# Differential attention on one core: value and output tiles turned in 32x32 squares by VectorE instead of 128x128 by TensorE

## What is computed

```
h = rms_norm(x, norm_pre) * (1 + scale) + shift           # scale, shift, gate from silu(c) @ ada_w + ada_b
q, k, v, z = h @ w_in                                      # four slices of 2048 columns
p1, p2 = softmax(q1 k1' * s), softmax(q2 k2' * s)          # chunk-causal mask, chunks of 64
o = (p1 - lam * p2) @ v                                    # per head, 256 wide
o = rms_norm(o, subln) * (1 - lambda_init) * silu(z)
out = x + gate * rms_norm(o @ w_out, norm_post)
```

## Time and profile before

| what | value |
|---|---|
| device time, median of 3 runs | 1906.76 us (1906.63 to 1907.32) |
| profiled execution, its own time | 1907.34 us |
| profiled execution, span of the trace | 1905.5 us |
| PE busy | 1866.0 us (98%) |
| DVE busy | 1379.5 us (72%) |
| ACT busy | 810.1 us (43%) |
| POOL busy | 794.4 us (42%) |
| DMA queue of SP, share of 16 engines | 76.4% |

### The profile page before, as it was taken

How to read it: one execution, slowest core, us unless ns; L and a number is a source line. 1 busy time by engine, 2 the same in 40 slices (tenths; PEclk the granted TensorE clock), 3 DMA queues, 4 the chain that set the end, 5 groups by cost and what they waited for, 6 DMA issues and landing times.

```text
span 1905.5 us, 26384 instructions
## 1 busy us (share of the span) xinstructions
PE 1866.0 (98%) x9072; PEld 1540.9 (81%) x9072; DVE 1379.5 (72%) x2028; ACT 810.1 (43%) x1516; POOL 794.4 (42%) x844
## 2 busy tenths in 40 slices
PE   4999999999999999999999999999999999999998
PEld 1488888888888888888888888888888888888886
DVE  3687888886655546787887877878778776569467
ACT  5633333333444433444443444444444445546452
POOL 2076565655644523344344434434443422116023
PEclk9999999999999999999999999999999999999999
DMA  9898898886674698786877778686777679657777
GB/s 354 253 313 279 274 297 278 284 290 232 214 267 160 237 356 263 225 250 192 253 229 227 235 216 252 198 254 212 232 240 221 213 228 291 207 186 257 258 240 265
DMA packets 394048, 473.16 MB, mean 248 GB/s; under 512 B 22614, under 2 KB 268476, under 8 KB 391228
## 3 DMA queue, kind: packets, MB, share of 16 engines
q1 hardware_dynamic: 393632, 471.43, 76.4%
q10 hardware_dynamic: 284, 0.05, 0.0%
HBM read 323.54 MB, written 147.86 MB: 247 GB/s over the span
## 4 chain that ended last, share of the span: by engine, by line
PE 93%; DVE 1%; DMA 1%; ACT 0%; issue 0%; SPq 0%; POOL 0%; DVEq 0%; POOLq 0%; ACTq 0%
PE ps L1752 30%; PE ps L1754 30%; PE ps L1753 30%; PE ps L1885 2%; PE ps L1861 1%; PE ps L1904 1%; PE ps L1721 0%; DMA ubf<-s_dr 0%; DMA z_dr<-cc 0%; PE ps L1833 0%; DVE ring L1310 0%; ACT h L1040 0%; DVE xt L1632 0%; DVE tB L1330 0%; DVE tB L1327 0%
## 5 line engine op out<-in xcount | busy, mean ns | idle before, releaser
L1752 PE MATMUL ps<-blk,ring 128*128 128x512 f32 x1524 | 603.3, 396 | 2.6 <-DVE blk L1357 1.9
L1754 PE MATMUL ps<-blk,ring 128*128 128x512 f32 x1524 | 594.6, 390 | 0.0
L1753 PE MATMUL ps<-blk,ring 128*128 128x512 f32 x1524 | 594.2, 390 | 0.0
L1752 PEld LDWEIGHTS ps<-blk,ring 128*128 128x128 f32 x1524 | 286.3, 188 | 66.0 <-issue 9.7
L1754 PEld LDWEIGHTS ps<-blk,ring 128*128 128x128 f32 x1524 | 286.0, 188 | 60.8
L1753 PEld LDWEIGHTS ps<-blk,ring 128*128 128x128 f32 x1524 | 286.5, 188 | 55.8
L1310 DVE TENSOR_TENSOR ring<-sums,ring 128x512 fp32r<-128x512 f32 x256 | 234.7, 917 | 95.5 <-ACT ring L1006 93.6
L836 POOL TENSOR_TENSOR sums<-raw 128x512 f32<-128x512 f32 x128 | 191.5, 1496 | 226.9 <-DVE ring L1310 206.0
L1006 ACT ACTIVATE ring<-sums 128x512 fp32r<-128x512 f32 x256 | 160.6, 628 | 179.3 <-PE ps L1754 175.6
L1310 DVE TENSOR_TENSOR ring<-raw,ring 128x512 fp32r<-128x512 f32 x192 | 179.2, 934 | 58.9 <-ACT ring L1006 58.5
L836 POOL TENSOR_TENSOR sums<-sums,raw 128x512 f32<-128x512 f32 x128 | 190.2, 1486 | 20.8 <-DVE ring L1310 14.3
(11 more groups left out here) (159 smaller groups left out, 3181.7 us busy)
## 6 DMA issues: line engine op xcount, KB each, us to landing
raw<-in_diff_w_in_dram SPq DMA_DIRECT2D x64, 1024.0 KB, 7.8
d_dr<-cc SPq DMA_DIRECT2D x124, 256.0 KB, 3.2
cc<-d_dr SPq DMA_DIRECT2D x124, 256.0 KB, 4.1
ubf<-s_dr SPq DMA_DIRECT2D x113, 256.0 KB, 5.0
ada<-in_ada_w_dram SPq DMA_DIRECT2D x88, 256.0 KB, 7.3
tb<-in_diff_w_out_dram SPq DMA_DIRECT2D x32, 512.0 KB, 5.5
t_dr<-tb SPq DMA_DIRECT2D x32, 512.0 KB, 4.9
ada<-in_ada_w_dram SPq DMA_DIRECT2D x32, 512.0 KB
```

The source lines that it names most:

```text
L1752: MM(dst, a_hi, b_hi, start=start, stop=False, skip_group_check=True)
L1753: MM(dst, a_hi, b_lo, start=False, stop=False, skip_group_check=True)
L1754: return MM(dst, a_lo, b_hi, start=False, stop=stop, skip_group_check=True)
```

## The change

Nothing is transposed across the whole of 128 partitions any more. DVE's transpose turns each square of 32x32 in its place, and the DMAs put the squares where they belong.

- `v_turn` is now a DVE instruction of 512 columns from `cc` into bank VX, one slot after the product, in `posts`; `v_dr` keeps rows of 512 tokens, so the stores of values have runs of 2 KB where they had 512 bytes. `load_v` is four DMAs of 32 partitions, each of 16 x 32 runs of 128 bytes, and is issued after the block's first slot.
- `o_turn` is gone from PE. `gate` transposes `o_sb` with a DVE instruction of 256 columns and multiplies by `z_sb` with one instruction; the factor `subln` is now `sub_row`, multiplied in `out_scale`.
- `ozf` and `osum` are one tile `o_all`. `store_pair` is four DMAs of 32 partitions, each 32 x 32 runs of 128 bytes; in the blocks of the first seven heads two of them are issued ahead of the first slot and two ahead of the second slot of the odd block after the pair's second one.
- `load_z` is four DMAs of 8 x 32 runs of 128 bytes, issued by ACT in those blocks (by SP in the last head).

```diff
-        v_dr = dram("v_dr", [HEADS * SEQ, 2, VD])
+        v_dr = dram("v_dr", [HEADS * 2, 2, 2, P, HALF])
-        s_dr = dram("s_dr", [8, HEADS, P, PAIRS, P])
+        s_dr = dram("s_dr", [HEADS, 8 * P, PAIRS, P])
...
             def load_v(h, qb):
-                sp.dma_start(v_sb[:, qb].bitcast(F32),
-                             v_dr[h * SEQ + qb * P:h * SEQ + (qb + 1) * P]).then_inc(v_ld[qb % 2], 16)
+                for c in range(0, P, SIDE):
+                    n = qb % HT * P + c
+                    sp.dma_start(v_sb[c:c + SIDE, qb].rearrange("i s (c j) -> i (s c) j", j=SIDE).bitcast(F32),
+                                 v_dr[h * 2 + qb // HT, :, :, :, n:n + SIDE].rearrange(
+                                     "s m (c i) j -> i (s m c) j", i=SIDE)).then_inc(v_ld[qb % 2], 16)
...
-            def store_pair(h, p):
+            def store_pair(h, p, pieces=range(0, P, SIDE)):
                 sp.wait_ge(ozf_ok, h * NB + 2 * p + 2)
-                sp.dma_start(s_dr[0:4, h, :, p].rearrange("o p n -> p o n"),
-                             ozf.rearrange("p i m n -> p (i m) n")).then_inc(s_st, 16)
                 sp.wait_ge(osum_ok, 4 * (h * PAIRS + p + 1))
-                sp.dma_start(s_dr[4:8, h, :, p].rearrange("o p n -> p o n"), osum[:, :, :]).then_inc(s_st, 16)
+                for c in pieces:
+                    sp.dma_start(s_dr[h, :, p, c:c + SIDE].rearrange("(o j) i -> j o i", j=SIDE),
+                                 o_all[c:c + SIDE].rearrange("j o (b i) -> j (o b) i", i=SIDE)).then_inc(s_st, 16)
...
-                    load_v(h - 1, qb)
                     load_qk(*divmod(a + 1, NB))
-                    for _ in range(sum(SPREAD[qb])):
+                    for k in range(sum(SPREAD[qb])):
+                        if a > 1 and a % 2 and k < 2:
+                            store_pair((a - 2) // NB, (a - 2) % NB // 2, (0, SIDE) if k == 0 else (2 * SIDE, 3 * SIDE))
                         slot(n)
                         n += 1
+                        if k == 0:
+                            load_v(h - 1, qb)
...
-                    load_z(h - 1, qb)
-                    if a and a % 2 == 0:
-                        store_pair((a - 1) // NB, (a - 1) % NB // 2)
...
+            def v_turn(n):
+                i, pi = divmod(n, NP)
+                h, o = head_part(i)[0], AT[pi]
+                if h or o:
+                    dve.wait_ge(post_d, 12 * h + o if o else 12 * (h - 1) + 4)
+                dve.wait_ge(ev_d, 3 * GP + NP * (i - GP) + pi + 1)
+                V.transpose(ps[:, VX], cc[:, buffer_of(i, BLOCK[pi])]).then_inc(vt_ok, 1)
...
             def gate(h, qb):
                 a = h * NB + qb
+                dve.wait_ge(o_ok, a + 1)
+                V.transpose(ps[:, OB, VD:2 * VD], o_sb[:, :]).then_inc(oT_done, 1)
+                dve.wait_ge(z_ld, (a + 1) * 16 * (P // SIDE))
+                if a > 1:
+                    dve.wait_ge(s_st, PAIR_STORED * (a // 2))
                 dve.wait_ge(oT_done, a + 1)
-                dve.wait_ge(z_ld, (a + 1) * 16)
-                if a > 1:
-                    dve.wait_ge(s_st, 32 * (a // 2))
-                for m in range(2):
-                    i = STT(ozf[:, a % 2, m], ps[:, OB, VD + m * P:VD + (m + 1) * P], sub8[:, m:m + 1],
-                            z_sb[:, m], ALU.mult, ALU.mult)
-                i.then_inc(ozf_ok, 1)
+                TTV(ozf[:, a % 2], ps[:, OB, VD:2 * VD].rearrange("p (m n) -> p m n", m=2), z_sb[:, :, :],
+                    ALU.mult).then_inc(ozf_ok, 1)
...
-            def v_turn(i, pi):
-                h, _ = head_part(i)
-                b, o = BLOCK[pi], AT[pi]
-                pe.wait_ge(*read_out(i, pi))
-                if h or o:
-                    pe.wait_ge(post_d, 12 * h + o if o else 12 * (h - 1) + 4)
-                for t in range(HT):
-                    last = TR(ps[:, VX, t * P:(t + 1) * P], cc[:, buffer_of(i, b), t * P:(t + 1) * P], ident[:, :])
-                last.then_inc(vt_mm, 1)
...
-            def o_turn(h, qb):
-                a = h * NB + qb
-                pe.wait_ge(o_ok, a + 1)
-                for m in range(2):
-                    last = TR(ps[:, OB, VD + m * P:VD + (m + 1) * P], o_sb[:, m * P:(m + 1) * P], ident[:, :])
-                last.then_inc(oT_done, 1)
```

More of the change, by code:

```diff
@@ L218, in build @@
         o_sb = at("o_sb", [P, VD], F32, z_at)
-        ozf = at("ozf", [P, 2, 2, P], F32, z_at)
-        osum = at("osum", [P, 4, P], F32, z_at)
+        o_all = at("o_all", [P, 8, P], F32, z_at)
+        ozf, osum = o_all[:, 0:4].rearrange("p (t m) n -> p t m n", t=2), o_all[:, 4:8]
         assert z_at[0] == e2_at[0]
@@ L526, in store @@
                     if part == 2:
-                        dst = v_dr[h * SEQ + half * HALF:h * SEQ + (half + 1) * HALF].rearrange("(t p) s d -> p t s d", p=P)
-                        sp.dma_start(dst[:, :, s, m * P:(m + 1) * P],
-                                     src.rearrange("p (t d) -> p t d", t=HT).bitcast(F32)).then_inc(stored[o], 16)
+                        sp.dma_start(v_dr[h * 2 + half, s, m], src.bitcast(F32)).then_inc(stored[o], 16)
                     else:
@@ L1009, in _ @@
             act.wait_ge(c_in, 16)
-            A(cexp[:, :], craw[:, :], ACT.Exp, scale=-1.0).then_inc(c_e, 1)
+            A(cexp[:, :], craw[:, :], ACT.Exp, scale=-1.0).then_inc(c_ok, 1)
             for t in range(TT):
@@ L1172, in before, with load_z @@
                 return divmod(a - 1, NB)
+            def load_z(h, qb):
+                a = h * NB + qb
+                if qb == 0:
+                    for e in range(4):
+                        act.wait_ge(stored[e], (h * 4 + 4) * 32)
+                if a > 0:
+                    act.wait_ge(ozf_ok, a)
+                for c in range(0, P, SIDE):
+                    act.dma_start(z_sb[c:c + SIDE].rearrange("j m (b i) -> j (m b) i", i=SIDE),
+                                  z_dr[h * 2:h * 2 + 2, :, qb * P + c:qb * P + c + SIDE].rearrange(
+                                      "m (b j) i -> j (m b) i", j=SIDE)).then_inc(z_ld, 16)
             def unit_high(n):
@@ L1202, in _ @@
                         n += 1
+                    load_z(h - 1, qb)
                     if a + 1 == LH * NB:
@@ L1294, in _ @@
             TTV(lamp[:, 1:2], cols[:, R_LAM + 2:R_LAM + 3], cols[:, R_LAM + 3:R_LAM + 4], ALU.mult).then_inc(lam_p, 1)
-            V.tensor_scalar(sub8[:, :], cols[:, R_SUB:R_SUB + 2], (1.0 - LAMBDA_INIT) / 2, None, ALU.mult).then_inc(cols_ok, 1)
             dve.wait_ge(lam_e, 1)
@@ L1501, in posts @@
                         post_low(w)
+                if n - 1 >= NA and (n - 1) % NP in BLOCK and head_part((n - 1) // NP)[1] == 2:
+                    v_turn(n - 1)
             def maxes(h, qb, m):
@@ L1557, in _ @@
                 take(n)
+            dve.wait_ge(sub_in, 16)
+            V.tensor_scalar(sub_row[:, :], sub_row[:, :], (1.0 - LAMBDA_INIT) / 2, None, ALU.mult).then_inc(cols_ok, 1)
             n = NA + PARTS_IN * NP
@@ L1844, in slot @@
             def slot(n, js=range(KB)):
-                if js.start == 0 and n - 2 >= NA and (n - 2) % NP in BLOCK:
-                    f, fp = divmod(n - 2, NP)
-                    h, part = head_part(f)
-                    if part == 2:
-                        v_turn(f, fp)
                 if n < NALL:
                     product(n, js)
-            def v_turn(i, pi):
-                h, _ = head_part(i)
-                b, o = BLOCK[pi], AT[pi]
-                pe.wait_ge(*read_out(i, pi))
-                if h or o:
-                    pe.wait_ge(post_d, 12 * h + o if o else 12 * (h - 1) + 4)
-                for t in range(HT):
-                    last = TR(ps[:, VX, t * P:(t + 1) * P], cc[:, buffer_of(i, b), t * P:(t + 1) * P], ident[:, :])
-                last.then_inc(vt_mm, 1)
             def scores(h, qb, m):
@@ L1921, in _ @@
                         n += 1
-                    if a:
-                        o_turn(*before(a))
                     cut = 1 if qb == HT - 1 else 0
@@ L1972, in _ @@
                     scores(LH, qb, 1)
-                o_turn(*((LH, qb - 1) if qb else (LH - 1, NB - 1)))
                 for i in range(n1):
@@ L1982, in _ @@
             tick(u + 1)
-            o_turn(LH, NB - 1)
             for v in range(u + 2, BEGIN[LAST]):
```

38 lines of the change are left out of this document (22 added, 16 removed).

## The result

The changed kernel runs in 1991.38 us (median of 4 runs, 1987.72 to 1992.57), the kernel before beside it in 1907.04: 1.0437 times as long, 95% interval 1.0419 to 1.0456. The prediction said 1919, 1888 to 1955, slower with 0.62. The direction was right, the size wrong by 72 us.

The account below looks back on a forecast made before the run. PE, busy for 98% of the span, was taken as the bound. 24 us gained from moved transposes against 37 lost to gate's new wait made 1907.3 + 13 = 1920, 1919 against the median; range 1888 to 1955.

Parts of the forecast that it names:

- the gain of 24: On PE: us expected to come in from moving the transposes to DVE, 28 less about 4.
- What leaves PE: PE's stream: 128 + 128 transposes gone, 28 us, less about 4 where prob comes late; 24 left.
- where `prob` is only 0.1 us early: Blocks qb = 3, 6 and 1 in seven heads: o_turn's time becomes a wait, about 4 us off the gain.
- What DVE takes on: DVE: transposes at 0.7 us (512 columns) and 0.4 (256), 22 us plus 13 more for gate; 80% busy becomes 84 to 85%.
- Below 100% it costs PE nothing by itself: Woven stretch: DVE's added work, at 84 to 85% busy, is covered by its waits for PE's products.
- ACT issues four DMAs a block, 4 x 0.45, at the end of the last slot, 322.7 of 750 us busy: hidden: ACT's gate loads at the end of a block's last slot: four issues at 0.45 us, expected to cost nothing.
- the 8300 rows that I named as a sign: PE's profile: with L1861 and L1904 gone, 8300 rows were expected to be left.
- a wait of 37: gate's wait for the pair's store: 24.5 us at qb = 3, 11 at qb = 1, 1 at qb = 7.
- What the DMAs take on: DMA engines: 327,680 small packets at 11 to 14 ns, 80 to 140 us more; 75% busy becomes 84 to 91%, still fitting.
- The wait that appears: gate in odd blocks waits for the pair's store; weighted 3.5 us later at qb = 3, 1.9 at qb = 1.
- the pair lands in time: Rival, 0.28: only issue and latency count, packets don't queue as summed; faster, 1886 to 1901 us, middle 1893.
- small packets make the DMA engines the bound of the whole stretch: Rival, 0.12: packets cost more; at 28 ns 124% load and about 2120 us, at 18 ns 1973.

Follow-up runs that it names:

- e15: e5 with the products' DMA issued ahead of the wait for the sums and the pair's stores behind the odd block's first slot: 1895.39 us, 0.9949 of the kernel before.
- e5: e4 with every fine DMA made plain, VectorE's turns kept, squares left unplaced: 1908.63 us, 1.0006 of the kernel before.
- e6: Kernel before, TensorE's turns kept, with the fine DMAs for values, gates and pairs, squares ending in other places: 1971.72 us, 1.0338 of the kernel before.
- e4: Changed kernel with gates loaded by SP, whole pair stored at the even block's end, values loaded ahead of queries and keys: 1970.93 us, 1.0337 of the kernel before.
- e9: e4 with still four DMAs each, but pieces of 2 KB (values) and 512 bytes (gates, pairs), unplaced: 1933.00 us, 1.0137 of the kernel before.
- e2: Changed kernel with the gates' four loads issued by SP at the block's end instead of by ACT: 1995.26 us, 1.0464 of the kernel before.
- e1: Changed kernel with all four DMAs of a pair issued at the end of the even block: 1958.40 us, 1.0287 of the kernel before.
- e16: Kernel before, turns on TensorE and its own DMAs, with a pair's two stores behind the odd block's first slot: 1919.61 us, 1.0063 of the kernel before.

## Why the prediction was wrong

Three terms carry the 72 us: the issues of the fine DMAs, for which the sum had no term; the gain of 24, of which at most 11 came over the kernel before; and the lower clock behind waits, which was left out.

**What leaves PE, 28 - 4 = 24: mis-sized.** Cleared of the DMAs (e15) it is 11 us in the time. PE's busy time falls by 24.5 us against before. Its idle time grows by 12.4 (1893.4 - 1841.5, against 39.5). The step that failed is "where `prob` is only 0.1 us early": I read three blocks a head. Between before and e15 the table shows no gain at qb = 1 and 6, 0.2 us at qb = 0, 4, 5 and 7, 0.7 at qb = 2, and 0.3 lost at qb = 3. PE's weight load waits for `prob` 29 times in e15, 15.4 us in sum (2.4 in the kernel before). What leaves a bound engine is only a gain in the blocks where its partner isn't at its heels.

**What DVE takes on: right in size, wrong in effect.** The two transposes in the changed kernel's groups by line (us in sum, mean ns, idle before):

```profile
L1559 DVE STREAM_TRANSPOSE ps<-o_sb 128x256 f32<-128x256 f32 x64 | 28.5, 445 | 0.0
L1526 DVE STREAM_TRANSPOSE ps<-cc 128x512 f32<-128x512 f32 x32 | 23.1, 722 | 0.6
```

0.7 and 0.4 were taken. "Below 100% it costs PE nothing by itself" failed: in e5, which has the turns on DVE and plain DMAs, `prob` and the pair's sums come late, as shown. (PE keeps 8816 instructions, not the 8300 rows that I named as a sign.)

**"ACT issues four DMAs a block, 4 x 0.45, at the end of the last slot, 322.7 of 750 us busy: hidden": wrong.** A share of busy time over a stretch isn't the cover at a place. The issues took 201 x 0.59 us between 790 and 1530, up to 3.9 for four in a row, ahead of `square` on the path to `prob`; and at qb = 1 they stand behind another engine's store. I had named no instruction behind them in ACT's order. SP's are the same mistake at larger scale: the prediction counted the pair's DMAs in the engines' queue and priced packets, but gave the issues, twenty for every six, 0.4 to 0.55 us each only in the rival. This is the step that cost most: e6 and e4 put the fine DMAs at 64 and 62 us, where the sum had a wait of 37.

**What the DMAs take on: right in sum, wrong in meaning.** Packets grew by 253,075 (246,000 expected), the DMA share of the woven stretch from 0.75 to 0.84 (84 to 91%). q1 and q10 took 80.9% of 16 x 1985.9 us, before 76.4% of 16 x 1905.5, so 151 us more for each engine, where 80 to 140 stood; with the 145 that it replaces this is 14.4 ns for a piece of 128 bytes (151 + 137 + 8 = 296 us x 16 / 327,680), the upper value of the two I had. A rival hung on the Trainium skill's 512 bytes (DMA: Bandwidth & Descriptors, Specifications): smaller transfers are read-modify-write. The trace agrees only that a small piece is dear for its bytes (half of the 28.4 ns of 512), not that stores double: the gates' loads alone (q10, 55,488 packets for 5.9% of 16 x 750 us) took 12.8 ns each, and 14.4 is the mean with the stores in it. I concluded "it still fits". On average it did; in bursts the engines were full, for in the changed kernel their share is about 1.0 from 3 to 12 us behind the start of qb = 3. What had no place in the sum is the row of issues. The Trainium skill (DMA: Bandwidth & Descriptors, Rules for kernel authors) says of two transfers to disjoint halves of the partitions: don't bother. e9, with four quarters, agrees: 24 us for that alone. The Trainium skill (DMA: Bandwidth & Descriptors, Issuing engines are not separate DMA queues) also says that the sequencer's time to start a DMA is usually small relative to the DMA. For one DMA the trace agrees, 0.62 us against 4.1 to landing; in sum it isn't small, 562 of 740 us in e4.

**The wait that appears.** At qb = 3 3.5 us were forecast, and the block grew by 5.0 (the product of `gate` 0.8 later than forecast, then the lower clock). That `gate` waits there was right; what made it wait was the row of issues more than the engines' queue. At qb = 1 1.9 us were forecast, and it grew by 2.75. How much of this is ACT's in-order wait isn't settled, since it stays when SP issues the gates (14.1 in e2), and 1.0 of it goes with the pair issued early (e1). qb = 2, 4, 5 and 7 were given 0.2 us a head in all; compared with e15 they cost 0.7, 0.9, 0.8 and 0.7. Against before it is 9 us a head and 64 in the seven; some 19 more come in the last woven block (24.4 us where it was 17.6) and behind it, in the last head, of which the prediction didn't speak, and 3 came off ahead of the first block.

**The clock: missing.** For the same 8816 instructions PE is busy for 1868.9 us in the changed kernel, for 1845.4 in e5 and for 1841.5 in e15, so 23 to 27 us of the loss are slower matmuls. Summed up from windows of 0.5 us, PE was granted the lower level for 51 us in the changed kernel, none of it ahead of the woven stretch, and for 4 in the kernel before. At 0.21 us for 0.12, 51 us at the lower level lose some 22: an estimate, and near the other. A us of waiting cost PE more than a us.

**The rivals.** That the pair lands in time is refuted. That small packets make the DMA engines the bound of the whole stretch is refuted: 0.84 busy, 14 ns. In the burst of qb = 3 they were full, and no run here tells how much of the 38 us of the small pieces that is. That what costs is the issuing of them, on both rows, was none of mine.

## What to carry to other kernels

Count the DMAs that an edit adds on each issuing engine, price them from that engine's row where it is fullest, and follow the row to the last thing in it that somebody waits for: a load that the edit doesn't touch can be the one that comes late. Before a turn is moved off a bound engine, look up in every block who arrives just ahead of it, for only the blocks with slack pay. And try the parts of such a change apart with plain DMAs and unplaced data: the square of four kernels settled what the trace of the changed kernel alone didn't.

## What the runs showed of the hardware

Four issues of `v_sb` in a row took 1.7 to 3.2 us on SP with pieces of 2 KB (e9) and 1.9 to 6.9 with pieces of 128 bytes (e4 and the changed kernel). Why (full queues, or the making of descriptors) isn't settled. Behind a wait of 4 us TensorE went on at granted clock 1.00 for 0.9 us and then at 0.50 for some 3.4, and with 24 idle transposes in the wait it fell in one of seven heads where it had fallen in six, which saved 1.4 us a head. Storing a pair one slot into the odd block instead of ahead of it, in the kernel before, which waits for hardly anything, cost 13 us (e16).
